# The oldest key tile of the window branch in a unit of its own, in a hybrid decoder layer's local attention

## The reference

```python
def window_attend(q, q_pos, k, v, k_pos, rel_bias):          # the window branch
    s = einsum(q, k) * HD_A ** -0.5
    dist = q_pos[:, :, None] - k_pos[:, None, :]
    bias = rel_bias[rel_bucket(dist)]                         # constant for dist >= 128
    valid = (dist >= 0) & (dist < WINDOW) & (k_pos >= 0)      # WINDOW = 512
    p = masked_softmax(s + bias, valid)
    return einsum(p, v)
...
o_a = gates[..., 0:1] * o_cmp + gates[..., 1:2] * o_sel + gates[..., 2:3] * o_win
```

## Time and profile before

| | us |
|---|---|
| median of three runs | 1117.63 |
| lowest and highest run | 1115.32, 1119.17 |
| the profiled execution | 1116.44 |
| its span in the profile | 1114.3 |
| TensorE busy in the span | 1074.0 |
| VectorE busy | 618.8 |
| ScalarE busy | 359.9 |

### The profile page before, as it was taken

How to read it: one execution, slowest core, us unless ns; L and a number is a source line. 1 busy time by engine, 2 the same in 40 slices (tenths; PEclk the granted TensorE clock), 3 DMA queues, 4 the chain that set the end, 5 groups by cost and what they waited for, 6 DMA issues and landing times.

```text
span 1114.3 us, 22552 instructions
## 1 busy us (share of the span) xinstructions
PE 1074.0 (96%) x8364; PEld 768.0 (69%) x8364; DVE 618.8 (56%) x1613; ACT 359.9 (32%) x875; POOL 88.9 (8%) x192
## 2 busy tenths in 40 slices
PE   6899999999999999998999999999999999999997
PEld 2455599998886687777876766764545476777775
DVE  0635323463423477767676666742324588888883
ACT  0422001121112475545455555631112123333330
POOL 0210100110000111100101010011000200000000
PEclk8999999999999999999999999999999999999997
DMA  9933260011006230000000000005794367788881
GB/s 350 314 114 95 79 204 2 16 35 56 1 1 123 55 106 1 1 1 1 2 1 2 1 1 1 1 1 120 162 316 150 135 220 267 268 273 290 276 216 57
DMA packets 96612, 120.25 MB, mean 108 GB/s; under 512 B 31569, under 2 KB 65380, under 8 KB 95480
## 3 DMA queue, kind: packets, MB, share of 16 engines
q1 hardware_dynamic: 96504, 118.81, 34.5%
HBM read 104.41 MB, written 14.36 MB: 107 GB/s over the span
## 4 chain that ended last, share of the span: by engine, by line
PE 84%; issue 8%; SPq 3%; DVE 3%; ACT 1%; DMA 1%; POOL 0%; ACTq 0%; POOLq 0%; DVEq 0%
PE PS L548 19%; PE PS L2047 10%; PE PS L1736 7%; PE PS L1714 7%; PE PS L1690 6%; PE PS L540 4%; PE PS L2549 3%; PE PS L1677 3%; PE PS L1711 3%; PE PS L2511 2%; PE PS L2562 2%; PE PS L1686 2%; PE PS L1242 1%; PE PS L647 1%; SPq L376 1%
## 5 line engine op out<-in xcount | busy, mean ns | idle before, releaser
L548 PE MATMUL PS<-AR 128*128 128x256 f32 (+2 forms) x896 | 219.7, 403 | 0.0
L548 PEld LDWEIGHTS PS<-AR 128*128 128x128 f32 x896 | 167.8, 190 | 45.2 <-issue 6.2
L1736 PE MATMUL PS<-CA,AR 128*128 128x128 f32 x704 | 112.2, 282 | 0.2 <-ACT AR L1790 0.2
L2047 PE MATMUL PS<-AR 128*128 128x512 f32 x256 | 112.3, 592 | 0.0
L962 DVE TENSOR_TENSOR AR<-PS,AR 128x256 f32<-128x256 f32 (+2 forms) x80 | 36.2, 453 | 134.0 <-PE PS L548 133.9
L1806 ACT ACTIVATE AR<-PS 128x512 f32<-128x512 f32 (+1 forms) x108 | 58.2, 546 | 138.6 <-PE PS L1736 137.9
L1736 PEld LDWEIGHTS PS<-CA,AR 128*128 128x128 f32 x704 | 77.9, 144 | 34.9 <-issue 25.8
L1714 PE MATMUL PS<-AR 128*128 128x65 f32 (+1 forms) x768 | 99.6, 270 | 0.0
L1714 PEld LDWEIGHTS PS<-AR 128*128 128x128 f32 x768 | 94.2, 192 | 0.2
L1790 ACT ACTIVATE AR<-PS,SM_ 128x512 f32<-128x512 f32 (+4 forms) x208 | 83.6, 475 | 17.8 <-DVE SM_ L1871 10.2
L2047 PEld LDWEIGHTS PS<-AR 128*128 128x128 f32 x256 | 47.5, 190 | 54.0 <-issue 54.0
(11 more groups left out here) (360 smaller groups left out, 1574.3 us busy)
## 6 DMA issues: line engine op xcount, KB each, us to landing
AR<-in_cache_nsa SPq DMA_DIRECT2D x128, 256.0 KB, 4.7
AR<-in_cache_mla SPq DMA_DIRECT2D x128, 96.0 KB, 3.6
AR<-in_x_prompt SPq DMA_DIRECT2D x16, 512.0 KB, 4.6
AR<-in_w_ada SPq DMA_DIRECT2D x3, 2048.0 KB, 11.8
AR<-in_w_in SPq DMA_DIRECT2D x6, 1024.0 KB, 8.7
AR<-in_w_ada SPq DMA_DIRECT2D x8, 512.0 KB, 4.4
AR<-in_w_out SPq DMA_DIRECT2D x4, 1024.0 KB, 11.4
AR<-in_w_out SPq DMA_DIRECT2D x2, 2048.0 KB, 17.5
```

Of the source, the lines that this page charges most:

```text
L548: mm = pe.matmul(bank[:, 0:WIDE[g]], tokens[:, k, :], w, start=(fresh and k == 0), stop=(last and k == 3), skip_group_check=True)
L1736: mm = pe.transpose(PS[:, 4 + c % 2, P * (t - t0):P * (t - t0) + P], tile(u, t), ident)
L2047: mm = pe.matmul(PS[0:n, 2 + 2 * (m % 2) + c, :], YTO[m % 2][:, f, 0:n], weights[:, f, 512 * c:512 * c + 512], start=(f == 0), stop=(f == 7))
```

## The change

For window groups with i of 4 or more, each half gets a unit of kind "old" ahead of its two window units. It has four heads (both r of the half, both g) and one key tile, the oldest, and takes one score slot. It has no exponentials and no chunks. VectorE adds the mask to its four score tiles, writes them to BTX[:, h, 256:384] in SBUF (oldest), and reduces them to one minimum a head, in EM. The window units compute the scores of four key tiles only, in one slot. VectorE reduces the far two tiles of both heads in one instruction, takes the minimum with EM, and merges 256 columns a head in place of 384. The exponential of the oldest tile reads SBUF. A window unit still has ten probability tiles (MANY), in three chunks, and the third is copied by ScalarE, the second by VectorE.

The order and the waits follow from the lists. TensorE's scores that follow a unit in two slots in a single slot wait for all four of its exponentials, those that follow a window unit for its first two, those that follow an old unit for VectorE's s_old. The choice between the two places of expo is made by the slots of neighbouring units that have exponentials (WHOLE). Window groups of tile 4 become crossed. GpSimd no longer writes the mask.

```diff
-            for h in range(H):
-                pool.tensor_copy(BTX[:, h, 256:384], wmask).then_inc(s_btw, 1)
...
+                if kind == "win" and i >= 4:
+                    UNITS.append(("old", i, half, [(r, g) for r in (2 * half, 2 * half + 1) for g in range(G)], k0, 1, len(GROUPS)))
...
-            if nb > 4:
+            if nb > 4 and kind != "win":
...
-            PSLOTS.append([(turn + n) % 4 for n in range(len(SLOTS[u]))])
+            PSLOTS.append([(turn + n) % 4 for n in range(0 if kind == "old" else 2 if nb > 4 else 1)])
...
+        MANY = [unit[5] > 4 for unit in UNITS]
+        OLD = [unit[0] == "old" for unit in UNITS]
+        WHOLE = [u for u in range(N) if not OLD[u]]
+        NTH = [sum(not old for old in OLD[:u]) for u in range(N)]
...
-            BY_A += [k < (1 if n == 3 else (n + 1) // 2) for k in range(n)]
+            BY_A += [k != 1 if kind == "win" and n == 3 else k < (1 if n == 3 else (n + 1) // 2) for k in range(n)]
...
-        TURNS_BACK = [kind in ("sel", "win") and i >= 5 for kind, i, half, last in GROUPS]
+        TURNS_BACK = [kind == "sel" and i >= 5 or kind == "win" and i >= 4 for kind, i, half, last in GROUPS]
...
+            if OLD[u]:
+                return 1024 * SLOTS[u][0] + 512 * (gi % 2) + P * (gi // 2)
...
-                return [(0, k0 + 1, 4), (512, k0, 1)]
+                return [(0, k0 + 1, 4)]
...
-            if before >= 0:
-                pe.wait_ge(s_exp, EXP0[before] + 2 if split else EXP0[before + 1])
+            if before >= 0 and OLD[before]:
+                pe.wait_ge(s_old, sum(OLD[:before + 1]))
+            elif before >= 0:
+                pe.wait_ge(s_exp, EXP0[before] + 2 if split or MANY[before] and not TWO[before] else EXP0[before + 1])
...
+                    r, g = heads[gi]
+                    sc = BTX[:, R * g + r, 256:384] if kind == "win" and lo else PSF[:, o + lo:o + hi]
...
-            early = lambda v: v < N and len(SLOTS[v]) == 1 and len(SLOTS[v - 1]) == 1
+            early = lambda u, v: len(SLOTS[v]) == 1 and len(SLOTS[u]) == 1
             expo(0)
-            for u in range(N):
-                if early(u + 1):
-                    expo(u + 1)
+            for u, v in zip(WHOLE, WHOLE[1:] + [None]):
+                if v is not None and early(u, v):
+                    expo(v)
                 for c in CH_OF[u]:
                     for og in OUT_AT[c]:
                         out_copy(og)
                     if BY_A[c]:
                         evac(act, c, lambda o, i: act.activation(o, i, ACT.Copy), s_evA)
-                if u + 1 < N and not early(u + 1):
-                    expo(u + 1)
+                if v is not None and not early(u, v):
+                    expo(v)
...
+            def oldest(u):
+                _, i, half, heads, k0, nb, og = UNITS[u]
+                dve.wait_ge(s_qk, QK0[u + 1])
+                past = [v for v in WHOLE if UNITS[v][0] == "win" and UNITS[v][1:3] == (i - 1, half)] if i > 4 else []
+                if past:
+                    dve.wait_ge(s_exp, EXP0[past[-1] + 1])
+                kept = BTX[:, :, 256:384].rearrange("p (g r) c -> p g r c", g=G)[:, :, 2 * half:2 * half + 2, :]
+                dve.tensor_tensor(kept, scores(u, 0, 0, 1024).rearrange("p (g r c) -> p g r c", g=G, c=P)[:, :, 0:2, :],
+                                  wmask.rearrange("p (g r c) -> p g r c", g=1, r=1).to_broadcast([P, G, 2, P]), ALU.add)\
+                    .then_inc(s_old, 1)
+                dve.wait_ge(s_old, sum(OLD[:u + 1]))
+                dve.tensor_reduce(EM[:, 4 * half:4 * half + 4].rearrange("p (r g) -> p g r", g=G), kept, AX, ALU.min)\
+                    .then_inc(s_mx, 1)
+                far_count[0] += 1
...
-                near = {"cmp": 64, "mla": P, "sel": min(256, P * nb),
-                        "win": min(256, P * nb) if i < 4 else 384}[kind]
-                far = 0 if kind == "cmp" else P * nb - near
+                if NTH[u] >= 2:
+                    dve.wait_ge(s_exp, EXP0[WHOLE[NTH[u] - 1]])
+                nm = NM[:, NTH[u] % 2, 0:len(heads)]
+                kept = kind == "win" and i >= 4
+                near = {"cmp": 64, "mla": P, "sel": min(256, P * nb), "win": min(256, P * nb)}[kind]
+                far = 0 if kind == "cmp" else P * (nb - kept) - near
...
+                    if kept:
+                        r2 = heads[0][0] % 2
+                        dve.tensor_tensor(nm, nm, EM[:, 4 * half + 2 * r2:4 * half + 2 * r2 + 2], ALU.min).then_inc(s_mx, 1)
+                        far_count[0] += 1
+                        dve.wait_ge(s_mx, far_count[0])
...
-                for og in FIN_AT[CH_OF[u][0]]:
+                for og in FIN_AT[CH_OF[u][0]] if CH_OF[u] else []:
...
```

More of the change, by code:

```diff
@@ L257, in build @@
         NM2 = small(2)
+        EM = small(8)
         NM = small(16).rearrange("p (s g) -> p s g", s=2)
@@ L1551, in build @@
                 holds[s] = u
-            PSLOTS.append([(turn + n) % 4 for n in range(len(SLOTS[u]))])
+            PSLOTS.append([(turn + n) % 4 for n in range(0 if kind == "old" else 2 if nb > 4 else 1)])
             PPREV.append([pholds[p] for p in PSLOTS[u]])
-            turn += len(SLOTS[u])
+            turn += len(PSLOTS[u])
             for p in PSLOTS[u]:
                 pholds[p] = u
-            EX0.append(EX0[u] + len(heads))
+            EX0.append(EX0[u] + (0 if kind == "old" else len(heads)))
         TWO = [len(s) == 2 for s in SLOTS]
+        MANY = [unit[5] > 4 for unit in UNITS]
+        OLD = [unit[0] == "old" for unit in UNITS]
+        WHOLE = [u for u in range(N) if not OLD[u]]
+        NTH = [sum(not old for old in OLD[:u]) for u in range(N)]
         QK0, EXP0 = [0], [0]
@@ L1566, in build @@
         for u, (kind, i, half, heads, k0, nb, og) in enumerate(UNITS):
-            tiles = 2 if kind == "cmp" else len(heads) * nb
+            tiles = 2 if kind == "cmp" else 0 if kind == "old" else len(heads) * nb
             CH_OF.append([])
@@ L1689, in pe_scores @@
                         keys = KSELT if kind == "sel" else KWINT
-                        mm = pe.matmul(scores(u, gi, o, o + P * n), QT[rg, r, q], keys[rg, ks], start=True, stop=True)
+                        mm = pe.matmul(scores(u, gi, o, o + P * n), QT[64 * g:64 * g + 64, r, q], keys[64 * g:64 * g + 64, ks],
+                                       start=True, stop=True)
                 if TWO[u] or m == len(runs) - 1:
@@ L1775, in expo @@
                 kind, i, half, heads, k0, nb, og = UNITS[u]
+                at = NTH[u] % 2
                 n = 64 if kind == "cmp" else P * nb
@@ L1822, in dve_attention @@
             far_count = [0]
+            def oldest(u):
[12 more added lines that the diff above has]
+                far_count[0] += 1
             def extremes(u):
+                if OLD[u]:
+                    return oldest(u)
                 kind, i, half, heads, k0, nb, og = UNITS[u]
                 dve.wait_ge(s_qk, QK0[u] + 1)
-                if u >= 2:
-                    dve.wait_ge(s_exp, EXP0[u - 1])
-                nm = NM[:, u % 2, 0:len(heads)]
-                near = {"cmp": 64, "mla": P, "sel": min(256, P * nb),
-                        "win": min(256, P * nb) if i < 4 else 384}[kind]
-                far = 0 if kind == "cmp" else P * nb - near
+                if NTH[u] >= 2:
[4 more added lines that the diff above has]
+                far = 0 if kind == "cmp" else P * (nb - kept) - near
                 if far:
@@ L1917, in dve_finish @@
             else:
-                if TURNS_BACK[og] and TWO[last]:
+                if TURNS_BACK[og] and MANY[last]:
                     dve.tensor_tensor(TOT[og % 4][:, 0:4], TOT[og % 4][:, 0:4], TOT[og % 4][:, 4:8], ALU.add).then_inc(s_cl, 1)
-                    dve.wait_ge(s_cl, 2 + sum(TURNS_BACK[o] and TWO[GROUPS[o][3]] for o in range(og + 1)))
+                    dve.wait_ge(s_cl, 2 + sum(TURNS_BACK[o] and MANY[GROUPS[o][3]] for o in range(og + 1)))
                 dve.reciprocal(RC, o[:, :, 64] if not TURNS_BACK[og] else TOT[og % 4][:, 0:4]).then_inc(s_rc, 1)
```

16 lines of the change are left out of this document (7 added, 9 removed).

## The result

The changed kernel takes 1153.2 us in the median (four runs, 1150.6 to 1158.6) against 1116.5 for the kernel before (four runs, one more than the prediction had): a ratio of 1.0337, 95% interval 1.0286 to 1.0389. Its profiled execution took 1151.24 us, with a span of 1149.2. It is 3.4% slower, where 1155 was forecast. TensorE is busy 1081.0 us, 7 more than in the earlier trace rows, and the span is 34.9 longer: the time is idle time of TensorE, for the most part.

A forecast was written before the change was run, and what follows sets the result against it. TensorE was taken as the bound, so only its own time and waits count. The profiled 1116.44 us plus 27.8 of waits and 10.5 of half clock gave 1154.7, against the median 1155.9; forecast 1155, range 1137 to 1168.

The forecast's parts named there:

- The chain: In window units of tiles 4 to 7: scores, minima, four exponentials, then the copy the ninth transpose needs; 5.40 us.
- The sum without the clock: Added time of tiles 4 to 7: 21.4 us for tiles 5 to 7, 6.4 for tile 4, together 27.8.
- the first old scores: At the last selected unit's head, waiting for four exponentials: +0.65 us at tiles 5 to 7, +0.05 at tile 4.
- The second MLA scores: Third copy on ScalarE delays the first MLA exponentials, so these scores wait 0.56 us longer in four tiles.
- Tile 4: Its window units, now crossed, and the waits around them were to cost 6.4 us more.
- The clock: Half clock behind seven of TensorE's twelve new waits, 1.5 us each: 10.5 us, within 0 to 20.
- The clock stays: Rival: the waits come in tiles 4 to 7 but the clock stays at 2.4 GHz: 1145 us, chance 0.25.
- The first copy isn't late: Rival: no late copy at the ninth transpose; 1116.5 us, chance 0.05, or 1112.5 with other waits hidden, chance 0.03.
- The price of a read from SBUF: ScalarE's exponential of the masked oldest tile: between nothing and 0.1 us each, taken at nothing.

The follow-up runs named there:

- The first experiment: Changed kernel, with ScalarE copying a window unit's first chunk before the next unit's exponentials: 1123.2 us, ratio 1.0069.
- the second: Kernel before, with only ScalarE's order changed: next window unit's exponentials ahead of this one's copies in tiles 4 to 7: 1144.0 us, ratio 1.0244.
- The third experiment: Changed kernel, with 14 unused transposes ahead of the ninth transpose of the window units that wait: 1145.0 us, ratio 1.0254.
- the sixth to ninth: Changed kernel, copy first and third copy on VectorE: 1121.4 us; plus two waits mended: 1113.8; that with tile 4 plain: 1113.5; or output copy earlier: 1112.5.
- the ninth: Changed kernel, first copy before exponentials, third copy on VectorE, first old scores awaiting three exponentials, output's copy after the first exponential: 1112.5 us, ratio 0.9978.
- the fourth and fifth experiments: Changed kernel with a window unit's third copy on VectorE: 1147.6 us; kernel before with tile 4's window groups crossed: 1117.5 us.

## Why the prediction was right

**The chain.** Each of its terms stands in the profile after: 1.17 to VectorE's start (1.18 read), 0.73, 0.19 (0.20), 0.59, four exponentials 669.36 to 671.47, 2.11 (2.05), the copy and its hand-over 0.73 (0.65). From the scores at 666.68 to the ninth transpose at 672.20 are 5.52 us; 5.40 was the sum. The waits are twelve, 26.3 us in all, 2.57 in the longest (2.5), 1.64 in tile 4's w0 (1.6); one is only 1.23, at 620.17, because TensorE came there late at half clock. The first experiment takes the order away and the waits go, the second puts the order alone into the kernel before and they come.

**The sum without the clock.** 27.8 us were worked out. The third experiment, whose clock stayed at 2.4 GHz in the stretch, measures 27.7, and 28.4 without what the filler itself gave. Of the terms beside the chain, the first old scores wait 0.60 at tile 6 (0.65) and 1.19 at tile 5, where 0.28 was waited before. The second MLA scores wait 1.04 (0.5 + 0.56) at all four tiles; at tile 4 there was no such wait before, so that the whole 1.04 is new there, and its term was too small. Tile 4 costs 7.2 us (534.72 to 574.09 against 534.05 to 566.19) where 6.4 was worked out, the other three 21.2 together where 21.4 was.

**The clock.** It was taken as seven falls of 1.5 us, 10.5, with none to all as bounds. The profile has four stretches, 17.1 us at half clock by their edges, and they cost about 5.8. That half clock follows some of the waits was right, and the size too large: the number of stretches was a guess, and what decides it is still open. Equal waits of 2.56 us were followed by half clock at 752 and not at 551 or 558. The price of one held on average, 5.8 us in four are 1.45 each against 1.5 taken, though one of the four was twice as long (1.66 us at tile 5, since the next unit's wait was shorter for it, 2.67 for the two of tile 6, 1.47 at tile 7). That 1155 is within 2 us of the 1153.2 measured is partly luck. In the profiled execution the clock's term was 4.7 too large and the sum of the rest 0.6 too small. But that was one of the shorter executions (1151.2, of 1150.6 to 1158.6), and the medians differ by 36.7 us where its stretch differs by 34.2.

**The rivals.** "The clock stays" is the third experiment, with the filler in it, and it gave what was worked out for it, 1145.0 against 1145. "The first copy isn't late" (the fourth rival, which the prediction's text on the chain calls the third) is the first, and the sixth to ninth. Its condition, a wait below 0.3 us at the ninth transpose, holds there and nowhere in the change. Its gain was put too high: 1112.5 was 5 us less than 1117.6, while the best of these, the ninth, took 1112.5 beside a kernel before of 1116.1, and its stretch is 2.3 us shorter. And with the copy ahead but the output's copy still behind, the first experiment took 1123.2, where the rival had 1116.5.

**What was missed.** The output's copy behind the exponentials: in the changed kernel it costs nothing, since TensorE waits longer for the chunk's copy, but once that is mended it is the next wait, 7.4 us in seven places. The forecast of the first experiment left it out and was 3 us short. The price of a read from SBUF was taken at nothing: an exponential of 128 from SBUF takes 0.39 to the next step (670.70 to 671.09), against 0.34 from PSUM before:

```profile
...
658.08 0.36 ACT L1787 ACTIVATE AR<-PS,SM_ 128x128 f32<-128x128 f32 x1
...
658.42 0.37 ACT L1787 ACTIVATE AR<-PS,SM_ 128x128 f32<-128x128 f32 x1
...
```

The four exponentials came out 0.06 longer than taken, which the two reads from SBUF can account for, and the copy with its hand-over 0.08 longer; with the 0.02 that the first terms are shorter this is the 0.12 between the chain and its sum. The Trainium skill has 52 cycles of 1.2 GHz between the two sources (VectorE: DVE Perf Modes, "The TRN2 errata"), by estimate 0.04 us. The trace agrees, with 0.05.

## What to carry to other kernels

- When a unit's buffers get smaller, look for code that chooses its order by them. Here a test "both units take one slot" stood for "the scores are two units ahead", which was true of all units that it had applied to, and false of the new ones.
- On an engine that runs its list in order, a piece that frees a buffer for the bound engine goes ahead of a piece that waits for this very engine's newest result. Where both are short, put the one whose input is ready first.
- Mending the largest wait shows the next one: reckon the next by the same timeline, before expecting the full gain.

## What the runs showed of the hardware

Waits of TensorE of 2.0 to 2.6 us amid dense work are sometimes followed by half clock and sometimes not, for the same wait in the same program. The wait of 1.97 us that stands before 518.78 in the kernel before is in all eleven profiles; in nine half clock follows, in those of the fourth and fifth experiments it doesn't. With a filler that kept TensorE busy for 1.75 of some 2.5 us, no half clock followed the window units' waits (one profile). And the clock can be at half for longer and while TensorE is busy: in five of the nine experiments' profiles it was so for 10 to 14 us from 388 on, at the beginning of the attention, where this code is the same in all. Just ahead of it TensorE waits 1.2 us, with half clock behind and without (1.22 before 386.40 in the third experiment, 1.21 before 386.32 in the kernel before). These are windows of the same stretch, of the changed kernel and of the third experiment:

```profile
...
390.00:402.00 12.00, 11.23 (x93) 9.46 (x92) 8.91 (x46) 8.45 (x31) 1.46 (x2) 1.00 0.86 251
...
```

```profile
...
390.00:402.00 12.00, 12.00 (x58) 10.75 (x59) 6.14 (x27) 5.81 (x21) 0.07 (x1) 0.50 0.79 238
...
```

The first is the changed kernel, the second the third experiment: TensorE is busy 12.00 of 12.00 us there and gets 0.50. This moves an execution by some 4 us (tile 4's first old scores are at 539.17 in the third experiment and at 534.72 in the changed kernel). It is one part of what the runs of one kernel differ by; the time behind the stretch, 355.4 to 360.0 us, is another. That is why the stretch is compared above. What starts such falls isn't settled; no experiment was made on it.
